# Mixer gates: the pooled branch in three rounded passes, and a third of the modulation quarters made among the heads

## What is computed

```
# first block, mixer: four mLSTM heads and a pooled branch, then per output tile
merged = sigmoid(ga) * (yp @ w_br_a) + sigmoid(gb) * (og @ w_br_b)   # branches
x      = x + merged @ w_out
# yp = (window mean of u - u) @ w_pool * pool_scale,  windows 2, 4, 8, 16
# og = the heads' gated outputs

# second block, both layers
c_act = silu(c)
mod   = c_act @ w_ada[layer] + b_ada[layer]      # shift, scale, gate: 3 x 1024 values
```

## Time and profile before

| | us |
|---|---|
| median of 3 runs | 3371.98 (3370.2 to 3374.91) |
| the profiled execution, its own time | 3376.36 |
| its span | 3374.6 |
| TensorE busy | 3327.1 |
| VectorE busy | 2100.3 |
| ScalarE busy | 1599.5 |
| mixer: heads and pooled branch | to about 324 |
| eight output tiles | 324 to about 597 |

### The profile page before, as it was taken

One profiled execution on the slowest core, in us unless ns is written; L12 is line 12 of the kernel. 1 busy time (PEld: TensorE's weight loads), 2 busy tenths in 40 slices (PEclk: granted clock), 3 DMA queues, 4 the chain that ended last, 5 costly groups with the idle time before them and its releaser, 6 DMA issues. The chain is left out here.

```text
span 3374.6 us, 55706 instructions
## 1 busy us (share of the span) xinstructions
PE 3327.1 (99%) x23754; PEld 2759.9 (82%) x23754; DVE 2100.3 (62%) x2531; ACT 1599.5 (47%) x1887; POOL 313.7 (9%) x265
## 2 busy tenths in 40 slices
PE   9999999999999998999999999999999999999998
PEld 7887776778888887888888888888788888888887
DVE  7655543469898887756656663455666567753544
ACT  5342111248888785443356543533443356643432
POOL 0000000001011102000123210000000123120000
PEclk9999999999999999999999999999999999999999
DMA  6211551369999997122111111243122111111433
GB/s 236 77 58 47 175 166 65 140 231 399 413 415 416 414 413 298 49 76 88 52 52 64 43 66 50 94 186 127 64 75 88 58 46 58 39 64 51 156 125 112
DMA packets 97245, 492.94 MB, mean 146 GB/s; under 512 B 10921, under 2 KB 11433, under 8 KB 59105
## 3 DMA queue, kind: packets, MB, share of 16 engines
q1 hardware_dynamic: 77216, 417.31, 32.4%
q0 software_dynamic: 14160, 51.55, 4.4%
q10 hardware_dynamic: 5616, 20.45, 1.5%
HBM read 431.43 MB, written 57.84 MB: 145 GB/s over the span
## 5 line engine op out<-in xcount | busy, mean ns | idle before, releaser
L136 PE MATMUL ps<-HH,WS 128*128 128x512 f32 (+1 forms) x2592 | 1034.6, 399 | 4.5 <-DVE WS L1574 2.7
L138 PE MATMUL ps<-HH,WS 128*128 128x512 f32 (+1 forms) x2592 | 1013.3, 391 | 0.1
L137 PE MATMUL ps<-HL,WS 128*128 128x512 f32 (+1 forms) x1952 | 762.3, 391 | 0.0
L136 PEld LDWEIGHTS ps<-HH,WS 128*128 128x128 f32 (+1 forms) x2592 | 487.2, 188 | 112.6 <-DVE WS L1574 6.4
L138 PEld LDWEIGHTS ps<-HH,WS 128*128 128x128 f32 (+1 forms) x2592 | 486.9, 188 | 106.9 <-issue 0.5
L1639 ACT ACTIVATE WA<-ps 128x512 f32<-128x512 f32 x240 | 142.9, 596 | 864.4 <-PE ps L138 841.9
L137 PEld LDWEIGHTS ps<-HL,WS 128*128 128x128 f32 (+1 forms) x1952 | 367.0, 188 | 74.7 <-issue 1.5
L136 PE MATMUL ps<-WAR 128*128 128x512 f32 x768 | 306.8, 399 | 0.9 <-DVE WAR L1368 0.9
L138 PE MATMUL ps<-WAR 128*128 128x512 f32 x768 | 301.0, 392 | 0.0
L1574 DVE TENSOR_TENSOR WS<-RAW,WS 128x1024 fp32r<-128x1024 f32 (+2 forms) x152 | 201.9, 1329 | 117.8 <-ACT WS L1569 117.8
L827 DVE TENSOR_TENSOR WRR<-WR,WAR 128x2048 fp32r<-128x2048 f32 x107 | 241.3, 2288 | 34.7 <-ACT WAR L823 34.7
(11 more groups left out here) (416 smaller groups left out, 5310.3 us busy)
## 6 DMA issues: line engine op xcount, KB each, us to landing
WR<-in_weu SPq DMA_DIRECT2D x36, 1024.0 KB, 9.1
WR<-in_wed SPq DMA_DIRECT2D x36, 1024.0 KB, 9.0
WR<-in_weg SPq DMA_DIRECT2D x35, 1024.0 KB, 10.5
RAW<-in_wo SPq DMA_DIRECT2D x32, 1024.0 KB, 4.9
WA<-in_wada SPq DMA_DIRECT2D x48, 512.0 KB, 4.5
H<-in_weg SPq DMA_DIRECT2D x23, 1024.0 KB, 10.5
H<-in_weu SPq DMA_DIRECT2D x23, 1024.0 KB, 9.3
H<-in_wed SPq DMA_DIRECT2D x22, 1024.0 KB, 10.4
```

The source lines that it names most:

```text
L136: t.matmul(o, l[0], r[0], start=st, stop=False)
L137: t.matmul(o, l[0], r[1], start=False, stop=False)
L138: return t.matmul(o, l[1], r[0], start=False, stop=sp)
```

## The change

1. **Pooled branch in three passes.** The branch's operand `yp` gets a rounded part `yh`, written by ScalarE from PSUM, and VectorE writes the rest. Its half of the branch weights (512 columns) is split too: `br_hi` on ScalarE behind the copies of `ga`, `br_lo` on VectorE ahead of the split of the tile behind `gb`, in one of the three `wss` pieces. TensorE makes these products by `mm3`; the other branch stays as it was.
2. **Quarters among the heads.** Quarters 0 to 15 are loaded and accumulated in the heads: 0 to 3 behind `hm` of head 0, 4 behind `masked` of head 1, 5 to 8 behind `hm` of head 1, 9 behind `masked` of head 2, 10 to 13 behind `hm` of head 2, 14 and 15 behind `mdif` of head 3. SyncE's loads of the quarter three further on stand at the same steps of its own program.
3. **The rest in the first three output tiles.** Quarters 16 to 25, 26 to 36 and 37 to 47 belong to tiles 0, 1 and 2; five of each stand behind the tile's sum, the others among the passes of the next tile. Sums on TensorE: pieces 0 to 3 in the pass `u1`, 4 and 5 at tile 1, 6 and 7 at tile 2, 8 to 11 at tile 3.
4. The activation of the condition moves to head 0.

```diff
@@ vector_core, and the same points in plan_core and sync_core @@
+            vector_quarters(v, early("mdif", h))
             yield
...
+            vector_quarters(v, early("masked", h))
             free(v, wa, "m_KE", h)
...
                 v.scalar_tensor_tensor(out=half(og, i), in0=ps("zT", h, i), scalar=p1("g_head", h), in1=half(og, i), op0=ALU.mult,
                                        op1=ALU.mult).then_inc(*up("hm", h, i))
+            vector_quarters(v, early("hm", h))
             yield
@@ the schedule and SyncE's part @@
+        EARLIER = 16
+        EARLY = {("hm", 0): range(0, 4), ("masked", 1): range(4, 5), ("hm", 1): range(5, 9), ("masked", 2): range(9, 10),
+                 ("hm", 2): range(10, 14), ("mdif", 3): range(14, 16)}
+        def quarters(m):
+            return (range(16, 26), range(26, 37), range(37, 48))[m] if m < 3 else ()
+        def sums_of(m):
+            return ((), range(4, 6), range(6, 8), range(8, 12))[m] if m < 4 else ()
+        def sync_quarter(s, x):
+            free(s, wa, "wq", x)
+            if x >= AHEAD:
+                s.wait_ge(*at("mod_acc", (x - AHEAD) // 4, (x - AHEAD) % 4 * 2 + 1))
+            s.dma_start(tl("wq", x), ...)
+        def sync_core(s, h):
+            sync_quarters(s, early("mdif", h))
+            yield
+            sync_quarters(s, early("masked", h))
+            yield
+            if h == 0:
+                sync_first_quarters(s, 0)
+            yield
+            yield
+            sync_quarters(s, early("hm", h))
+            yield
@@ scalar_gates, vector_gates @@
+            free(a, wss, "br", m)
+            a.activation(branch_parts(m)[0], raw(M, source_no(f"ga{m}"))[:, 2048:2560], ACT.Copy).then_inc(*up("br_hi", m))
...
-                for x in quarters(m - 1)[4:]:
-                    vector_quarter(v, m - 1, x)
+                vector_quarters(v, quarters(m - 1)[5:])
             yield
+            hi, lo = branch_parts(m)
+            v.wait_ge(*at("br_hi", m))
+            v.tensor_tensor(lo, raw(M, source_no(f"ga{m}"))[:, 2048:2560], hi.bitcast(F32), ALU.subtract).then_inc(*up("br_lo", m))
@@ tensor_branches @@
-                        o = t.matmul(ps("br", m, j, i), w[:, j * 512 + k * 128:j * 512 + (k + 1) * 128], half(tl(nm, k), i),
-                                     start=k == 0, stop=k == 3)
+            t.wait_ge(*at("br_lo", m))
...
+                    o = mm3(t, ps("br", m, 0, i), (hi[:, ks], lo[:, ks]),
+                            (half(tl_rounded("yh", k), i), half(tl_rounded("yp", k), i)), k == 0, k == 3)
...
+                    o = t.matmul(ps("br", m, 1, i), w[:, k * 128:(k + 1) * 128], half(tl("og", k), i), start=k == 0, stop=k == 3)
@@ vector_pool @@
-                    v.tensor_scalar(half(tl("yp", gi), i), ps("yp", gi, i), p1("pscale", gi), None, ALU.mult)
+                    v.wait_ge(*at("yp_hi", gi, i))
+                    v.scalar_tensor_tensor(out=half(tl_rounded("yp", gi), i), in0=ps("yp", gi, i), scalar=p1("pscale", gi),
+                                           in1=half(tl_rounded("yh", gi), i).bitcast(F32), op0=ALU.mult, op1=ALU.subtract)
```

More of the change, by code:

```diff
@@ new lines, in plan_sums, with tensor_sums @@
+        def plan_sums(ns):
+            for n in ns:
+                brief("mod", n, end=("md", n))
+                if n % 2:
+                    wa.give(("acc", n // 2), ("mod_mm", n))
+        def tensor_sums(t, ns):
+            for n in ns:
+                free(t, banks, "mod", n)
+                t.wait_ge(*at("mod_acc", n, 7))
+                for q in range(4):
+                    o = t.matmul(ps("mod", n)[:, q:q + 1], half(tl("acc", n // 2), n % 2)[:, q * 128:(q + 1) * 128], ones[:, 0:1],
+                                 start=True, stop=True)
+                o.then_inc(*up("mod_mm", n))
@@ new lines, in vector_sums @@
+        def vector_sums(v, ns):
+            for n in ns:
+                layer, j = n // 6, n % 6
+                md = MD[:, layer * 32:layer * 32 + 32]
+                v.wait_ge(*at("mod_mm", n))
+                v.tensor_tensor(md[:, 4 * j:4 * j + 4], ps("mod", n)[:, 0:4], p2(layer, "b_ada", 4 * j, 4), ALU.add).then_inc(
+                    *up("md", n))
+                if j == 5:
+                    v.wait_ge(*at("md", n))
+                    v.scalar_tensor_tensor(out=md[:, 24:32], in0=md[:, 8:16], scalar=1.0, in1=p2(layer, "norm_g", 0, 8), op0=ALU.add,
+                                           op1=ALU.mult).then_inc(*up("mod_done", layer))
@@ new lines, in plan_quarters, with plan_first_quarters, sync_first_quarters @@
+        def plan_quarters(xs):
+            for x in xs:
+                if x % 8 == 0:
+                    wa.take("acc", x // 8)
+                wa.give(("wq", x), ("mod_acc", x // 4, x % 4 * 2 + 1))
+                if x + AHEAD < (EARLIER if x < EARLIER else 48):
+                    wa.take("wq", x + AHEAD)
+        def plan_first_quarters(x):
+            for y in range(x, x + AHEAD):
+                wa.take("wq", y)
+        def sync_first_quarters(s, x):
+            for y in range(x, x + AHEAD):
+                sync_quarter(s, y)
@@ L2981, in plan_core, with vector_quarters @@
+        def sync_core(s, h):
[3 more added lines that the diff above has]
+            yield
+            if h == 0:
+                sync_first_quarters(s, 0)
[3 more added lines that the diff above has]
+            yield
+        def vector_quarters(v, xs):
+            for x in xs:
+                vector_quarter(v, x)
         def plan_core(h):
             wa.take("E", M, h)
+            plan_quarters(early("mdif", h))
@@ L2991, in plan_core @@
             wa.take("m_KE", h)
+            plan_quarters(early("masked", h))
             for i in range(2):
@@ L3183, in plan_pool @@
                 next(steps)
+                if gi == 1:
+                    plan_sums(range(4))
                 if gi:
@@ L3229, in scalar_pool, with pooled @@
         def scalar_pool(a):
-            for gi in range(4):
-                yield from scalar_pass(a, M, tile_no(f"u{gi}"), ("u", gi))
-            yield from scalar_gates(a, 0)
+            def pooled(gi):
+                free(a, wa, "yh", gi)
+                for i in range(2):
+                    a.wait_ge(*at("yp_mm", gi, i))
+                    a.activation(half(tl_rounded("yh", gi), i), ps("yp", gi, i), ACT.Identity, scale=p1("pscale", gi)).then_inc(
+                        *up("yp_hi", gi, i))
+            for gi in range(4):
+                steps = scalar_pass(a, M, tile_no(f"u{gi}"), ("u", gi))
+                next(steps)
+                yield
+                next(steps)
+                if gi:
+                    pooled(gi - 1)
+                yield
+                next(steps, None)
+            gates = scalar_gates(a, 0)
+            next(gates)
+            yield
+            next(gates)
+            yield
+            next(gates)
+            pooled(3)
+            yield
+            yield from gates
         def vector_pool(v):
@@ L3338, in plan_branches @@
                 raws.take("raw", M, x + 2)
[L3339 to L3351, removed]
-        def sync_branches(s, m):
[L3354 to L3363, removed]
+            plan_sums(sums_of(m))
+            plan_quarters(quarters(m))
+        def sync_branches(s, m):
             x = source_no(f"ga{m}")
@@ L3366, in sync_branches @@
                 sync_raw(s, M, x + 2)
-            for x in quarters(m):
-                if x + AHEAD < 48:
-                    quarter(x + AHEAD)
+            sync_quarters(s, quarters(m))
         def tensor_branches(t, m):
[L3372 to L3378, removed]
-                        o = t.matmul(ps("br", m, j, i), w[:, j * 512 + k * 128:j * 512 + (k + 1) * 128], half(tl(nm, k), i),
-                                     start=k == 0, stop=k == 3)
[L3381 to L3389, removed]
+            w = raw(M, source_no(f"ga{m}"))[:, 2560:3072]
+            hi, lo = branch_parts(m)
+            t.wait_ge(*at("br_lo", m))
+            for i in range(2):
+                free(t, banks, "br", m, 0, i)
+                for k in range(4):
+                    if m == 0:
+                        t.wait_ge(*at("yp", k, i))
+                    ks = slice(k * 128, (k + 1) * 128)
+                    o = mm3(t, ps("br", m, 0, i), (hi[:, ks], lo[:, ks]),
+                            (half(tl_rounded("yh", k), i), half(tl_rounded("yp", k), i)), k == 0, k == 3)
+                o.then_inc(*up("br_mm", m, 0, i))
+            for i in range(2):
+                free(t, banks, "br", m, 1, i)
+                for k in range(4):
+                    if m == 0:
+                        t.wait_ge(*at("hm", k, i))
+                    o = t.matmul(ps("br", m, 1, i), w[:, k * 128:(k + 1) * 128], half(tl("og", k), i), start=k == 0, stop=k == 3)
+                o.then_inc(*up("br_mm", m, 1, i))
+            tensor_sums(t, sums_of(m))
         def vector_branches(v, m):
@@ L3399, in vector_branches, with vector_quarter @@
```

(10 more changed lines are left out.)

39 lines of the change are left out of this document (30 added, 9 removed).

## The result

The changed kernel takes 3382.05 us (median of 13 runs, 3380.08 to 3386.7) against 3371.92 before: ratio 1.0032, 95% interval 1.0024 to 1.004. It is slower by 10.1 us; 9.5 was forecast. The total is close, but the part of it that the lower clock makes lies partly at other places than forecast.

A forecast was written before the change was run, and what follows sets the result against it. TensorE, busy 99% of the span, was taken as the bound. Terms -11.1 + 3.5 + 3.7 + 2.9 + 6.4 + 4.1 = +9.5 us, added to the median 3371.98, gave 3381.5 us; range 3367 to 3391.

The forecast's parts named there:

- Products: In eight output tiles, half the products go from fp32 to three passes: 1.39 us less a tile, -11.1 us in all.
- Work beside it: ScalarE's roundings, VectorE's rests, the moved activation and sums: 0, up to 1 us if a ScalarE copy comes late.
- Quarters in the tiles: VectorE's added quarters delay splits and br_lo: +1.5 us in tile 1, +1.0 each in tiles 2 and 3, +3.5 together.
- Quarters 0 to 4: Behind hm of head 0, covered by VectorE's idle time: cost 0, or 7.5 us without that cover.
- q3: Quarters 5 to 8 ahead of VectorE's split of q3 make TensorE wait +3.7 us (2.7 to 4.4).
- wpool: Its load, queued on SyncE behind those of quarters 13 to 15, makes TensorE wait +6.4 us ahead of u0 (5.4 to 10).
- The clock: TensorE at 1.2 GHz behind its two waits: +2.9 us behind q3 (0 to 4.4), +4.1 behind u0 (2.9 to 4.4).
- The sums: TensorE's modulation sums only move to other places in the kernel, at a cost of 0.

The follow-up runs named there:

- the kernel with half of the early quarters: Changed kernel with eight early quarters instead of 16, the others eight a tile over tiles 0 to 4, sums two pieces at a time: 3362.76 us, ratio 0.9976.
- the first four experiments: Single edits of the changed kernel: wpool loaded first, 3374.67 us; q3's split first, 3379.52; sums two pieces at a time, 3380.56; quarter 4 later, 3394.41.

## Why the prediction came out, step by step

- **Products (-11.1).** Right: 1.43 us a tile against 1.39, -11.4.
- **Work beside it (0).** Right but for the sums (below): in the kernel with half of the early quarters nothing new waits.
- **Quarters in the tiles (+3.5).** Right in sum. By starts of TensorE's instructions over the usual 0.23 us: 1.05, 0.87 and 0.84 ahead of `gb1` to `gb3`, 0.77 ahead of the branches of tile 3, 3.5 in all. By place the first was less than the 1.5 forecast, the others' splits more than 0.3: VectorE waited 2.46 us for a load ahead of the split in tile 2, where it had waited 1.47. The forecast wait of 0.7 at the branches of tile 2 stayed small.
- **Quarters 0 to 4 (0).** Right: no wait of TensorE between 100 and 200.
- **q3 (+3.7).** 2.9 us idle in the one profile, 3.4 in the other (3.0 and 3.6 by starts); the load of quarter 8 took 3.9 us in the first, not 4.5. Right within its bounds.
- **wpool (+6.4).** 6.3. `wpool` landed 5.1 us behind its issue instead of 4.5.
- **The clock (+2.9 and +4.1).** Right in its mechanism, mis-sized in its parts. Behind `u0` 5.4 us at 0.50, 2.7 lost, not 4.1. Behind `q3` nothing in one execution and 3.4 us at the lower level in the other, 1.7 lost; in the five profiles with a wait of 2.8 to 3.6 us there it fell in three. The 2.9 was also read wrongly from its own rows: the wait nearest to 3.7 is that of 4.16, whose price was 4.4, not that of 3.07; by it the sum would have been +11.0.
- **The sums (0, "only move").** This was wrong, and no row was given for it. They were not only moved but put together, four pieces where there had been two: 3.5 us of one-column matmuls at full clock, against runs of 1.70 behind which no fall stood. In the changed kernel's two profiles 7 and 3.4 us, and 7 us, are at the lower level at the sums: 5.1 and 3.5 lost. That a run of narrow matmuls can do this stood in the trace of the kernel before (L877, above).

So the total is right in part by luck: 7.0 us of clock were forecast behind two waits; about 3 to 4 came there, and 3 to 5 came at the sums, which the prediction had at nothing.

The executions bear out the share of the clock. The 13 runs of the changed kernel have a mean granted clock of 0.9916, the 22 of the kernel before that ran beside the first four experiments 0.9942 (each run's is given to three digits). A clock of c means 2 x (1 - c) of the span at the lower level, half of it lost: 28.4 us against 19.5, 8.9 more. The fixed terms make -11.4 + 3.5 + 3.0 + 6.5 = +1.6 (waits by starts), and with 8.9 that is 10.5, against 10.1 measured. My 7.0 comes near that, but it stood for two places only. The profiles agree: with the granted clock read in stretches of 1 us, 11.9 us are lost ahead of 640 in each of the changed kernel's two, against 3.4 in the kernel before. Of the 8.5 more, 3.4 stand at `u0` in both (with the end of the wait), the rest at the sums, and in the second also at `q3`.

"TensorE: Matmul & The Clock Gate" in the Trainium skill (HAM oscillation) fits the fall behind the wait of 6.3 us, which every profile with that wait shows. It says also, in Part 1, that the number of slow matmuls at a kernel's start varies from run to run; no run here shows that for the start, but a like variation shows at `q3`, where the two profiles of one kernel have a granted clock of 1.00 and 0.58.

**Open.** How much the sums cost in the mean of executions (1.5 us by the medians in one pair of kernels, 4.8 in another). Why the clock falls behind `q3` in some executions only; it doesn't follow the length of the wait (2.82 us with a fall, 3.62 without). The three-pass products with the old schedule of quarters weren't run. By my ledger their eight tiles of `mg` and four of `yh`, together with quarters up to tile 5, need more than the 22 pieces, which no run shows.

## What to carry to other kernels

When work is moved to an earlier stage "into idle time", look where that idle time lies against the next thing the bound engine needs: with the four quarters one instruction earlier TensorE waited 3 us, with them one later it did not wait. And follow the loads of the moved work through their issuing queue: here a small, unrelated load that had gone out 24 us ahead of its use became 6 us late, since it stood behind three waits. And when short work on the bound engine is moved, keep it in pieces as short as they were: here sums of 1.7 us in one run never brought the clock down, and sums of 3.5 us mostly did.

## What the hardware showed beyond expectation

- Waits of TensorE of 2.8 to 3.6 us at the same place among dense matmuls were followed by a fall of the clock in three of five profiles, and the longest of them was not (1.00 behind 2.89 and 3.62 us, 0.57 to 0.58 behind 2.82, 3.32 and 3.41).
- A run of 32 one-column matmuls back to back (3.6 us busy by the record at full clock) brought the clock to 1.2 GHz within it or shortly behind it at 11 of 14 places, as if it had been a wait: four records of fp32 matmuls took 2.8 us. Runs of 16 never did. The 32 matmuls of 36 columns (L877), which no edit touches, did it in 7 of 12 profiles.
- Loads of 512 KB on SyncE's queue landed in 7.4 us (median of five) where two row broadcasts of GpSimd ran among them, against 5.5 with one; the last of the five, with neither beside it, took 3.3. A freed piece decides when the broadcast starts.
